# Chunk-scan inverse factors turned by vector-engine block transposes, strip-wise mLSTM reads, row groups in turn

## The reference, cut to what matters

```python
# B, RWKV-7: per head a 64x64 state, per direction one scan over time
sa = jnp.einsum('bhvk,bhk->bhv', state, -kk_t)
state = state * w_t[:, :, None, :] + sa[..., None] * kka_t[:, :, None, :] + v_t[..., None] * k_t[:, :, None, :]
# C, S5: the inputs of the complex states, by group of 16 channels
bu = jnp.einsum('bsgc,gpc->bsgp', u_c, b_bar)
# D, mLSTM: gated scores of every query and key of a head, times the values and a row sum
s = jnp.einsum('bhcjd,bhcsd->bhcjs', q, k) * jnp.exp(log_intra - m_row[..., None])
num = jnp.einsum('bhcjs,bhcse->bhcje', s, v) + ...
h = num / jnp.maximum(jnp.abs(den), jnp.exp(-m_row))[..., None]
```

## Time and profile before

| what | value |
|---|---|
| three runs | 1927.68, 1924.59, 1920.54 us; median 1924.59 |
| the profiled execution | 1929.27 us, its span 1927.0 us |
| TensorE clock granted, mean | 0.988 of full speed |
| busy: TensorE, VectorE, ScalarE | 1857.4, 766.1, 332.7 us |

### The profile page before, as it was taken

How to read it: one execution, slowest core, us unless ns; L and a number is a source line. 1 busy time by engine, 2 the same in 40 slices (tenths; PEclk the granted TensorE clock), 3 DMA queues, 4 the chain that set the end, 5 groups by cost and what they waited for, 6 DMA issues and landing times.

```text
span 1927.0 us, 64702 instructions
## 1 busy us (share of the span) xinstructions
PE 1857.4 (96%) x29632; PEld 1647.3 (85%) x29632; DVE 766.1 (40%) x1790; ACT 332.7 (17%) x786; POOL 103.4 (5%) x44
## 2 busy tenths in 40 slices
PE   8998999999999999899998999999999999999997
PEld 6877887667777787788767999999999999999996
DVE  6987635211220398764524222232223222232224
ACT  3243312011100324341202000000000000000001
POOL 3600000000100160000000000000000000000000
PEclk9999999999999999999999999999999999999999
DMA  7323111534433332321174999999999999999992
GB/s 283 131 88 110 67 46 44 207 109 154 163 138 145 136 126 90 108 77 36 49 314 156 384 410 401 407 401 411 407 407 403 407 414 399 405 403 410 411 405 113
DMA packets 54476, 470.98 MB, mean 244 GB/s; under 512 B 5184, under 2 KB 5456, under 8 KB 20336
## 3 DMA queue, kind: packets, MB, share of 16 engines
q1 hardware_dynamic: 37744, 292.04, 39.1%
q10 hardware_dynamic: 16272, 175.06, 22.3%
q0 software_dynamic: 368, 2.64, 0.3%
HBM read 468.68 MB, written 1.05 MB: 244 GB/s over the span
## 4 chain that ended last, share of the span: by engine, by line
PE 84%; DVE 11%; issue 3%; ACT 2%; DMA 1%; SPq 0%; DVEq 0%; ACTq 0%
PE bank L1062 28%; PE bank L986 14%; PE bank L822 9%; PE bank L874 8%; PE bank L896 4%; PE bank L483 3%; PE bank L854 2%; PE bank L836 2%; PE bank L652 1%; PE bank L1013 1%; PE bank L1052 1%; PE bank L622 1%; DVE arena L1724 1%; DMA ring<-in_w_in 1%; PE bank L641 1%
## 5 line engine op out<-in xcount | busy, mean ns | idle before, releaser
L1062 PE MATMUL bank<-arena,ring 128*64 128x88 f32 x8192 | 335.4, 239 | 1.0 <-issue 1.0
L1062 PEld LDWEIGHTS bank<-arena,ring 128*64 128x64 f32 x8192 | 322.2, 137 | 1.2 <-issue 1.2
L1971 DVE TENSOR_TENSOR arena<-arena,bank 128x88 f32<-128x88 f32 x224 | 55.0, 246 | 544.7 <-ACT arena L1332 544.7
L1062 PE MATMUL bank<-arena 128*64 128x88 f32 x6144 | 246.1, 239 | 1.1 <-DVE arena L2014 1.1
L1062 PEld LDWEIGHTS bank<-arena 128*64 128x64 f32 x6144 | 238.0, 137 | 1.8 <-issue 1.3
L822 PE MATMUL bank<-xT,ring 128*128 128x256 f32 x1024 | 235.8, 390 | 0.7 <-issue 0.7
L822 PEld LDWEIGHTS bank<-xT,ring 128*128 128x128 f32 x1024 | 198.3, 196 | 33.4 <-issue 5.8
L1332 ACT ACTIVATE arena<-bank 128x88 f32<-128x88 f32 (+1 forms) x246 | 63.3, 257 | 931.9 <-PE bank L1062 738.2
L986 PE MATMUL bank<-arena,ring 128*64 128x88 f32 x4096 | 180.2, 239 | 1.5 <-issue 1.5
L986 PEld LDWEIGHTS bank<-arena,ring 128*64 128x64 f32 x4096 | 169.8, 137 | 4.9 <-issue 1.6
L483 PE MATMUL bank<-xT,ring 128*128 128x256 f32 x736 | 166.5, 389 | 3.9 <-DMA ring<-in_w_in 3.0
(11 more groups left out here) (407 smaller groups left out, 1667.6 us busy)
## 6 DMA issues: line engine op xcount, KB each, us to landing
ring<-in_moe SPq DMA_DIRECT2D x66, 1536.0 KB, 9.8
ring<-in_moe ACTq DMA_DIRECT2D x62, 1536.0 KB, 10.1
arena<-in_moe SPq DMA_DIRECT2D x49, 1536.0 KB, 9.8
arena<-in_moe ACTq DMA_DIRECT2D x47, 1536.0 KB, 9.8
ring<-in_ffn SPq DMA_DIRECT2D x22, 1536.0 KB, 6.6
ring<-in_w_gate SPq DMA_DIRECT2D x32, 1024.0 KB, 5.0
ring<-in_w_in SPq DMA_DIRECT2D x14, 1536.0 KB, 6.6
ring<-in_w_branch SPq DMA_DIRECT2D x8, 1024.0 KB, 4.9
```

Of the source, the lines that this page charges most:

```text
L1062: last = mm(bank[c:c + STRIP, g * CAP:(g + 1) * CAP], w[:, at:at + STRIP], rhs[:, kt, :], start=(kt == 0), stop=(kt == KT - 1), skip_group ...
L1971: tt_(ACTIVE_H[:, i, :], ff_sl[:, s % 2, 0:CAP], bank[:, CAP:2 * CAP], ALU.mult)\
```

## The change

It does four things.

1. On TensorE the products of level 0 and the bank `rwQ` are gone. VectorE now makes `rw_XT` only (in level 0 from `rw_CT` and the unit matrix), and turns it into `rw_X` with one `transpose` of 128x512 per direction in levels 0 to 4. This instruction turns each 32x32 block in its place. Up to level 4 the inverse has nothing outside its diagonal 32x32 blocks, so that is the whole transpose.
2. VectorE's order within a level: the adds and transposes come first, then `beside` of the next level, then the cut of the next level (`level_blocks`), which also waits until the P products that read `rw_CT` are done.
3. `reads(h)` uses stationary strips of 64 columns: 16 matmuls on two column halves of the array in turn, in place of 8.
4. `scores(j)` makes heads 2j and 2j+1 together, in two banks, with the lower and the upper row half in turn; the row sums are a function of their own. The S5 inputs go in two rounds of four banks, the four row groups in turn.

```diff
--- before.py
+++ after.py
@@ -610,31 +610,22 @@
                         gate(L, *FILL_GATES[lev])
                     if lev == ROWS_LEVEL + 1:
                         ml_rows(L)
+                    if lev == 0:
+                        continue
                     for d in range(2):
                         n = 12 * L + 2 * lev + d
                         pe.wait_ge(S["rw_CT"], n + 1)
-                        if lev:
-                            pe.wait_ge(S["rw_X"], 10 * L + 2 * (lev - 1) + d + 1)
-                        b = open_bank(("rwP", L, lev, d), "rw_P" if lev else "rw_X")
+                        pe.wait_ge(S["rw_X"], 10 * L + 2 * (lev - 1) + d + 1)
+                        b = open_bank(("rwP", L, lev, d), "rw_P")
                         for m in range(8):
                             for h in (0, 64):
-                                x = rw_X[h:h + 64, 8 * d + m, :] if lev else ident[h:h + 64, h:h + 64]
-                                last = mm(b[h:h + 64, m * 64:(m + 1) * 64], rw_CT[h:h + 64, 8 * d + m, :], x,
-                                          start=True, stop=True)
+                                last = mm(b[h:h + 64, m * 64:(m + 1) * 64], rw_CT[h:h + 64, 8 * d + m, :],
+                                          rw_X[h:h + 64, 8 * d + m, :], start=True, stop=True)
                         fill(last)
                     for d in range(2):
-                        if lev == 0:
-                            continue
                         n = 12 * L + 2 * lev + d
                         pe.wait_ge(S["rw_P"], n - 2 * L - 1)
                         pe.wait_ge(S["rw_XT"], n - 1)
-                        if lev < 5:
-                            b = open_bank(("rwQ", L, lev, d), "rw_X")
-                            for m in range(8):
-                                for h in (0, 64):
-                                    last = mm(b[h:h + 64, m * 64:(m + 1) * 64], rw_XT[h:h + 64, 8 * d + m, :],
-                                              rw_P[h:h + 64, 8 * d + m, :], start=True, stop=True)
-                            fill(last)
                         b = open_bank(("rwQT", L, lev, d), "rw_XT", n + 1)
                         for m in range(8):
                             for h in (0, 64):
@@ -706,13 +697,14 @@
 
                 pe.wait_ge(S[("pm_loaded", "pm2_loaded")[L]], 16)
                 pe.wait_ge(S["p_ready"], 12 * L + 1)
-                for i in range(S5T):
-                    h = 32 * (i % 4)
-                    b = open_bank(("bu", L, i), "s5_bu")
+                for q in range(2):
+                    b = [open_bank(("bu", L, 4 * q + i), "s5_bu") for i in range(4)]
                     for k, name in enumerate(("bre", "bim")):
-                        last = mm(two(b)[:, k, :], M(name, (i // 4) * P, P)[h:h + 32],
-                                  proj[h:h + 32, U0 + i // 4, 2:2 + T], start=True, stop=True)
-                    fill(last)
+                        for i in range(4):
+                            last = mm(two(b[i])[:, k, :], M(name, q * P, P)[32 * i:32 * i + 32],
+                                      proj[32 * i:32 * i + 32, U0 + q, 2:2 + T], start=True, stop=True)
+                            if k:
+                                fill(last)
 
             def s5_read(L, n):
                 d, half = n // 2, n % 2
@@ -765,13 +757,16 @@
                 fill(last)
                 pe.wait_ge(S["ml_qk"], L + 1)
 
-                def scores(h):
-                    o = 64 * (h % 2)
-                    b = open_bank(("mlS", L, h), "ml_S")
+                def scores(j):
+                    both = [open_bank(("mlS", L, 2 * j + i), "ml_S") for i in range(2)]
                     for st in range(2):
-                        last = mm(two(b)[:, st, :], ml_qk[o:o + 64, 2 + h // 2, st * P:(st + 1) * P],
-                                  ml_qk[o:o + 64, h // 2, :], start=True, stop=True)
-                    fill(last)
+                        for i, o in enumerate((0, 64)):
+                            last = mm(two(both[i])[:, st, :], ml_qk[o:o + 64, 2 + j, st * P:(st + 1) * P],
+                                      ml_qk[o:o + 64, j, :], start=True, stop=True)
+                            if st:
+                                fill(last)
+
+                def row_sums(h):
                     b = open_bank(("mlG", L, h), "ml_D")
                     for d in range(2):
                         r = 4 * d + h
@@ -785,14 +780,17 @@
                     for d in range(2):
                         for tt in range(TT):
                             for st in range(2):
-                                last = mm(b[:, (2 * d + tt) * 65:(2 * d + tt + 1) * 65],
-                                          ml_W[:, d, st, tt * P:(tt + 1) * P], ml_vt[:, st, h, :], start=(st == 0),
-                                          stop=(st == 1))
+                                for c in range(0, P, STRIP):
+                                    o = tt * P + c
+                                    last = mm(b[c:c + STRIP, (2 * d + tt) * 65:(2 * d + tt + 1) * 65],
+                                              ml_W[:, d, st, o:o + STRIP], ml_vt[:, st, h, :], start=(st == 0),
+                                              stop=(st == 1), skip_group_check=True)
                     fill(last)
 
                 scores(0)
+                row_sums(0)
                 rwkv_variance(L)
-                scores(1)
+                row_sums(1)
                 gate(L, 3, 0)
                 pe.wait_ge(S["ml_v"], L + 1)
                 for h in range(4):
@@ -801,8 +799,10 @@
                     branch(L, 1, (h,))
                     if h:
                         reads(h)
+                    if h == 0:
+                        scores(1)
                     if h < 2:
-                        scores(h + 2)
+                        row_sums(h + 2)
                         gate(L, 3, h + 1)
                 gate(L, 3, 3)
                 pe.wait_ge(S["ml_h"], 4 * (L + 1))
@@ -1629,26 +1629,35 @@
                                  b[:, :].rearrange("p (m c) -> p m c", m=4), bc(mask, 1, 4), ALU.mult), "rw_M",
                              hold=False)
                 dve.wait_ge(S["rw_M"], issued["rw_M"])
-                for lev in range(6):
+
+                def level_blocks(lev):
                     for d in range(2):
+                        if lev > 1:
+                            bank_of(dve, ("rwP", L, lev - 1, d))
                         dst = rw_CT[:, 8 * d:8 * d + 8, :]
                         src = rw_MM[:, 2 * d:2 * d + 2, :, 0, :].rearrange("p q c t -> p (q c) t")
                         step(tt_(dst, src, bc(C("lmask", (6 * d + lev) * CH, CH), 1, 8), ALU.mult), "rw_CT")
-                    beside(L, lev)
+
+                level_blocks(0)
+                for lev in range(6):
                     for d in range(2):
+                        x, xt = (flat(a[:, 8 * d:8 * d + 8, :]) for a in (rw_X, rw_XT))
+                        if lev:
+                            b = bank_of(dve, ("rwQT", L, lev, d))
+                            step(tt_(xt, b[:, :], xt, ALU.add), "rw_XT")
+                        else:
+                            step(tt_(rw_XT[:, 8 * d:8 * d + 8, :], rw_CT[:, 8 * d:8 * d + 8, :], bc(C("eye64"), 1, 8),
+                                     ALU.add), "rw_XT")
+                        if lev < 5:
+                            step(nc.vector.transpose(x, xt), "rw_X")
+                    if lev < 5:
                         if lev == 0:
-                            eye, r = bc(C("eye64"), 1, 8), slice(8 * d, 8 * d + 8)
-                            b = bank_of(dve, ("rwP", L, lev, d))
-                            step(tt_(rw_X[:, r, :], b[:, :].rearrange("p (m c) -> p m c", m=8), eye, ALU.add), "rw_X")
-                            step(tt_(rw_XT[:, r, :], rw_CT[:, r, :], eye, ALU.add), "rw_XT")
-                            continue
-                        if lev < 5:
-                            b = bank_of(dve, ("rwQ", L, lev, d))
-                            x = flat(rw_X[:, 8 * d:8 * d + 8, :])
-                            step(tt_(x, b[:, :], x, ALU.add), "rw_X")
-                        b = bank_of(dve, ("rwQT", L, lev, d))
-                        x = flat(rw_XT[:, 8 * d:8 * d + 8, :])
-                        step(tt_(x, b[:, :], x, ALU.add), "rw_XT")
+                            level_blocks(1)
+                            beside(L, 0)
+                            beside(L, 1)
+                        else:
+                            beside(L, lev + 1)
+                            level_blocks(lev + 1)
                 step(nc.vector.memset(flat(rw_S2[:, 0, :, :]), 0.0), "rw_S")
                 for s in range(NCH):
                     ch = (s, NCH - 1 - s)
```

## The result

The changed kernel takes 1901.18 us in the median of 4 runs (1899.0 to 1903.58), the kernel before 1924.82 us (1920.54 to 1927.68). The ratio is 0.9869, with a 95% interval of 0.9851 to 0.9887: 23.6 us or 1.3% less. The profiled execution took 1903.58 us with a span of 1901.3 us, 25.7 us under the span of before.

What follows compares the result with a forecast made beforehand. TensorE's own stream was taken as the bound. 2 x (6.9 + 3.2 - 0.3) + 2 = 21.6 us off the profiled 1929.3 gave 1907.7, a median of 1903; range 1894 to 1914.

Steps and rivals of the forecast that it cites:

- TensorE's stream is the bound, and what is saved ahead moves the expert stage: Expert stage: TensorE busy 200 of 200 us, never waiting for transfers, so time saved ahead moves the whole stage forward.
- The transpose, 0.70 us: VectorE's 128x512 transpose in the levels: 168 ns fixed plus 512 columns at 1.05 ns, all partitions at once.
- Both rivals on a slow transpose: VectorE's transpose by groups of partitions, 2.3 us, total 1915, chance 0.05; or block by block, 7.5 us, about 2004, chance 0.02.
- Levels, 6.9 us a layer: Chunk-scan levels 0 to 4: removed products gain 2.02 + 1.87 + 1.87 + 0.5 + 0.6 us, limited by cover.
- mLSTM, 3.2 us a layer: mLSTM reads and paired scores: 0.1 + 0.9 + 1.06 + 1.2 us arrive, nothing before the first second-branch product.
- the 0.1 us: mLSTM: gain from four scores taking the place of two, at 0.95 us for the four.
- The rival of strips that pay for loads: mLSTM reads: stationary loads run one after the other, reads gain nothing, 4.2 us back, total 1907; chance 0.10.
- the sequencer time that the prediction quotes: TensorE strips: skill's rule of about 62 ns per matmul when decoding in hardware is off; prediction set 40 ns a record against it.
- What does not arrive: mLSTM: 2.0 us becomes a gap before the first second-branch product; faster reads of head 2 bring only 0.3 us.
- S5 inputs, 0.3 us lost: S5 inputs: later ScalarE copies delay the S5 scans, a loss of 0.3 us a layer, between -0.5 and 0.5.
- Gaps of issue, 2 of 2.8 us: Level 1 of both layers: TensorE gaps of 1.98 and 0.80 us, of which 2 us were taken to go.
- The clock, zero: Half-clock stretches: as many drops saved as added, counted zero, with 5 us either way kept for the range.

Runs made afterwards that it cites:

- levels_only: Only the chunk-scan part of the change (inverse turned by VectorE, cut behind the mLSTM steps) on the kernel before: 1904.56 us, ratio 0.9885.
- s5_only: Only the S5 inputs in two rounds of four row groups, on the kernel before: 1927.99 us, ratio 1.0020.
- mlstm_only: Only the mLSTM part (strip reads, scores in pairs) on the kernel before: 1918.49 us, ratio 0.9959.
- turn_twice: The changed kernel with each block transpose done twice: 1907.57 us, ratio 0.9902 to the kernel before.
- cut_first: The changed kernel with the cut of the next level in front of the level's adds, from level 1 on: 1889.07 us, ratio 0.9805 to the kernel before.

## Why the prediction was right, point by point

The forecast was 1903 us, the measured time 1901.2; 21.6 us less were forecast and 23.6 measured. The mechanisms are those of the prediction, but that the number came so close is in part luck. The 21.6 us were counted on the profiled execution, and there the difference is 25.7 us. The points below are held against that, from start to start: levels 13.4 us (13.8 forecast), mLSTM 5.4 (6.4), gaps of issue 4.3 (2), bank wait 2.1 (none), S5 inputs 0.6 lost (0.6). That is 24.6 us; the last 1.1 us is what gained and lost stretches at half clock leave together, and is not split further.

- **TensorE's stream is the bound, and what is saved ahead moves the expert stage.** Right. The stage starts 27 us earlier (1010.13 in place of 1037.37, first row of L1062) and takes TensorE for 200 of 200 us again.
- **The transpose, 0.70 us.** Right, 0.712 us, by the way it was worked out: the fixed part of the 32x64 row plus one column per 1.05 ns. The Trainium skill (Vector Engine (DVE) Microarchitecture Reference, The reshape front-end and per-opcode configuration) has one reorder array in front of each bank of 32 channels. The trace agrees, now on 128 partitions: the four groups go together, since one after the other they would take 2.3 us. Both rivals on a slow transpose are out.
- **Levels, 6.9 us a layer.** Right. In layer 0, from the gate of level 0 to the scan, 75.0 us (194.24 to 269.26) became 63.3 us (196.28 to 259.57). Of the 11.7 us, 3.2 are gaps of issue (from start to start 2.3 in level 1, and 0.9 in the gate of level 3), 1.6 the half clock in the gate after the first, and 6.9 the levels. The two gates in the kernel before, where a gate without either takes 7.0 to 7.1 us from start to start:

```profile
220.24 8.67 PE L822 MATMUL bank<-xT,ring 128*128 128x256 f32 x32
...
234.58 0.48 PE L822 MATMUL bank<-xT,ring 128*128 128x256 f32 x1
235.72 6.96 PE L822 MATMUL bank<-xT,ring 128*128 128x256 f32 x31 [0.65 <-issue]
```

  Level by level: nothing waits in levels 0 to 2; P of level 3 waits 0.27 us and its product 0.54, which replace 0.72; P of level 4 waits 1.28 (1.4 forecast); before level 5 it is 2.85 (2.9). In layer 1 only 4.8 us arrive (71.2 us, 819.69 to 890.94, became 66.4, 804.62 to 871.06), because the half clock of levels 4 and 5 takes some 3 us back. `levels_only` has the same waits there at full clock and takes 63.6 us (805.89 to 869.48): 7.7 us less than before, 1.1 of it the gap of issue and 6.5 the levels.
- **mLSTM, 3.2 us a layer.** From the mean to the residual 68.2 us (293.01 to 361.17) became 61.0 us (283.31 to 344.35). Of the 7.1 us, 3.3 are two gates at half clock that now run at full, 1.1 (0.93 of it idle) is the bank wait, 2.7 the mLSTM. The two gates in the kernel before:

```profile
325.52 8.86 PE L822 MATMUL bank<-xT,ring 128*128 128x256 f32 x32
...
342.95 8.81 PE L822 MATMUL bank<-xT,ring 128*128 128x256 f32 x32
```

  The mechanism is right, and two sizes were a little off. A head's reads take 1.08 us, not 1.0, and took 1.83 from start to start before, so they give 0.75 and not 0.9. Four scores take 1.06 us, not 0.95, so the 0.1 us did not come. At 68 ns a strip the reads lie between the two rows that bounded them (60 and 80). The rival of strips that pay for loads is out. So is the sequencer time that the prediction quotes with it from the Trainium skill (TensorE: Matmul & The Clock Gate, Wait — 56ns, not 53.3ns?), if each record is one such matmul: the trace has 34 ns a record. Counted by matmuls of the program, two records each, it is 68 ns, which would not exclude it.
- **What does not arrive.** Right on both: what the first pair of scores and the reads of head 0 save (2.0 us forecast) became the gap of 1.84 us, and the gap before head 3 grew. There the forecast said 2.3 us in one place and an end 1.2 us earlier in another; measured are 1.73 us, grown from 1.52, and 1.1 us earlier.
- **S5 inputs, 0.3 us lost.** The sign and the mechanism are right: copies end 0.4 us later after the first matmul (5.57 in place of 5.17), and in `s5_only` TensorE reaches the late S5 read 0.1 us later in layer 0 and 0.5 in layer 1. On the time nothing finer than 1 or 2 us can be said.
- **Gaps of issue, 2 of 2.8 us.** All of it went, and 0.65 us that the sum had left out. The idle times are 3.4 us, from start to start 4.3. What TensorE waits for in these gaps no run shows; that they go with the shorter run of small matmuls is all that is seen.
- **The clock, zero.** Right in sum for the two profiled executions (0.988 and 0.988), and right in kind: three stretches around the gates of layer 0 gone with two in layer 1, and new ones, in levels 4 and 5 of layer 1 but not of layer 0, and also in stretches that the change leaves alone (0.83 in 185 to 195 us). Over all executions it was not zero: 36 of the kernel before have 0.9896 in the mean, the four of the changed kernel 0.9878. They ran at different times, so the difference is a hint only. It would be about 3 us lost, within the 5 kept for it, and would have hidden part of the 25.7 us.
- **Missed:** the bank wait, 1.9 us idle and 2.1 from start to start, which no row read showed as tied to the change. It and the gaps of issue, 2.3 us more than counted, outweigh the 1.4 us that mLSTM and levels fell short.

## What to carry to other kernels

Before counting a removed product, look at what covers the chain behind it: here levels 0 to 2 gave their products back in full because a gate covered the chain. Level 3 gave a quarter, since the next cut stood behind copies that can only follow the end of the gate, and level 4, which has no gate behind it, gave a third. When work is moved between engines, place what the next step waits for where the engine would idle anyway: moving one operation from behind the transposes to the front of them brought 3 us a layer, nearly half of what the levels had given. Faster matmuls ahead of a chain on another engine only lengthen a gap, and taking banks out of a rotation changes waits far from the edit, so the trace is worth reading there too.

## What the runs showed of the hardware

- A block transpose of 128x512 in float32 takes 0.71 us, nearly what an add of the same size takes (0.69), and doubling it adds just its length.
- Four matmuls on four row groups of 32 run together: eight of 256 columns took 1.07 us, where 16 took 3.34 us with two at a time. On two groups of 64 rows four took 1.06 us.
- The mean granted clock differs between executions of one kernel. Over 36 executions of the kernel before it lay between 0.988 and 0.993. Those at 0.988 took 1925.2 to 1930.5 us, those at 0.992 and 0.993 took 1919.1 to 1922.7, so 0.001 went with about 1.7 us. Nine executions of `mlstm_only` ranged from 0.986 to 0.993. One profile's clock therefore says little about a kernel.
- Three kernels do stand apart in all four of their executions: `turn_twice` at 0.986 to 0.987, the changed kernel at 0.987 to 0.988, `cut_first` at 0.991 to 0.992. The first has the longest gaps and the last the shortest. But `levels_only`, with the long gaps of the changed kernel, has 0.990 to 0.991, so the gaps are not the whole reason. In the profiles the levels of layer 1 fell to half clock in five of the six kernels with the gap of 2.6 us or more before level 5, and in none of the three with 0.70 us. In the changed kernel the fall came before that gap, behind one of 1.59 us, so the length of one gap alone does not decide it.
